# Key projections moved into the units of differential attention, and its values taken as 256 moving columns

## What is computed

```python
def diff_attention(q, k, v, cos, sin, lam_params, head_gain, lam_init):
    q = apply_rope(q, cos, sin)
    k = apply_rope(k, cos, sin)
    ...
        s = jnp.einsum('bqhcd,bkhcd->bhcqk', qb, k).astype(jnp.float32) * scale
        s = jnp.where(kpos[None, :] <= qpos[:, None], s, NEG_INF)
        p = jax.nn.softmax(s, axis=-1)
        a = p[:, :, 0] - lam * p[:, :, 1]
        return jnp.einsum('bhqk,bkhe->bqhe', a.astype(v.dtype), v)
    ...
    o = rmsnorm(o, head_gain) * (1.0 - lam_init)

def nsa(q, k_cmp, v_cmp, k_slc, v_slc, k_win, v_win, gate_logits, ...):
    kc = compress(k_cmp, cmp_pos[0], cmp_w1[0], cmp_w2[0])
    vc = compress(v_cmp, cmp_pos[1], cmp_w1[1], cmp_w2[1])
    ...
    ks = apply_rope(k_slc, cos, sin)
    kw = apply_rope(k_win, cos, sin)
```

## Time and profile before

| | |
|---|---|
| time, median of 3 runs | 2116.81 us (2115.66 to 2120.5) |
| the profiled execution: time | 2119.69 us |
| the profiled execution: span | 2117.9 us |
| mean granted TensorE clock over the span | 0.986 |
| TensorE busy | 2023.9 us (96%) |
| VectorE, ScalarE, GpSimd busy | 1041.1, 815.1, 275.3 us |

### The profile page before, as it was taken

How to read it: one execution, slowest core, us unless ns; L and a number is a source line. 1 busy time by engine, 2 the same in 40 slices (tenths; PEclk the granted TensorE clock), 3 DMA queues, 4 the chain that set the end, 5 groups by cost and what they waited for, 6 DMA issues and landing times.

```text
span 2117.9 us, 25446 instructions
## 1 busy us (share of the span) xinstructions
PE 2023.9 (96%) x10148; PEld 1697.5 (80%) x10148; DVE 1041.1 (49%) x1606; ACT 815.1 (38%) x1482; POOL 275.3 (13%) x272
## 2 busy tenths in 40 slices
PE   6999999999999999999998899989989999999998
PEld 6887888888878888888886788777777888888886
DVE  5665555555353222335545665856665543222333
ACT  5442443333243222324225643455554333222332
POOL 1001000000000000000013432266763000000000
PEclk9999999999999999999999899999999999999999
DMA  5232333333323332332541043311115423333332
GB/s 190 80 100 60 101 99 100 94 95 100 100 81 99 100 92 97 100 99 80 149 130 40 1 150 123 90 46 49 42 46 170 139 64 116 99 100 93 96 100 70
DMA packets 58982, 200.12 MB, mean 94 GB/s; under 512 B 8081, under 2 KB 8113, under 8 KB 58481
## 3 DMA queue, kind: packets, MB, share of 16 engines
q1 hardware_dynamic: 53936, 178.29, 27.3%
q0 software_dynamic: 4928, 20.21, 2.8%
HBM read 181.16 MB, written 8.39 MB: 90 GB/s over the span
## 4 chain that ended last, share of the span: by engine, by line
PE 75%; DVE 7%; ACT 5%; POOL 5%; issue 3%; DVEq 2%; DMA 1%; POOLq 1%; SPq 0%; ACTq 0%
PE ps L636 24%; PE ps L637 24%; PE ps L638 24%; POOL PU L592 5%; DMA raw<-in_w_all 1%; DVE Wl L1699 1%; DVE XN L1739 1%; DVE HTl L1748 1%; PE ps L1086 1%; ACT Pb L1367 1%; DVEq L2257 1%; POOLq L581 1%; PE ps L1002 1%; ACT XN L1240 1%; ACT Wh L1207 1%
## 5 line engine op out<-in xcount | busy, mean ns | idle before, releaser
L1699 DVE TENSOR_TENSOR Wl<-raw,Wh 128x1024 fp32r<-128x1024 f32 x307 | 377.4, 1232 | 766.3 <-ACT Wh L1207 764.9
L636 PE MATMUL ps<-HTh,Wh 128*128 128x512 f32 (+1 forms) x1696 | 642.8, 379 | 14.9 <-DVE HTl L1748 10.5
L637 PE MATMUL ps<-HTl,Wh 128*128 128x512 f32 (+1 forms) x1696 | 636.8, 375 | 0.0
L638 PE MATMUL ps<-HTh,Wl 128*128 128x512 f32 (+1 forms) x1696 | 636.7, 375 | 0.0
L1207 ACT CAST Wh<-raw 128x1024 fp32r<-128x1024 f32 x307 | 321.7, 1052 | 802.0 <-DMA raw<-in_w_all 802.0
L636 PEld LDWEIGHTS ps<-HTh,Wh 128*128 128x128 f32 x1696 | 321.7, 190 | 73.0 <-issue 13.6
L638 PEld LDWEIGHTS ps<-HTh,Wl 128*128 128x128 f32 x1696 | 321.1, 189 | 57.8
L637 PEld LDWEIGHTS ps<-HTl,Wh 128*128 128x128 f32 x1696 | 321.4, 190 | 55.1
L636 PE MATMUL ps<-Wh,Yh 128*128 128x512 f32 x528 | 206.1, 390 | 4.3 <-DVE Yl L1875 4.3
L638 PE MATMUL ps<-Wh,Yl 128*128 128x512 f32 x528 | 205.5, 389 | 0.0
L637 PE MATMUL ps<-Wl,Yh 128*128 128x512 f32 x528 | 205.4, 389 | 0.0
(11 more groups left out here) (281 smaller groups left out, 2382.2 us busy)
## 6 DMA issues: line engine op xcount, KB each, us to landing
raw<-in_w_all SPq DMA_DIRECT2D x307, 512.0 KB, 3.6
swp_d<-qkd SPq DMA_DIRECT2D x64, 64.0 KB, 2.9
g_dram<-gst SPq DMA_DIRECT2D x16, 256.0 KB, 4.0
ring<-g_dram POOLq DMA_DIRECT2D x16, 256.0 KB, 3.6
gpre<-in_g_pre POOLq DMA_DIRECT2D x5, 512.0 KB, 4.0
X<-in_x SPq DMA_DIRECT2D x4, 512.0 KB, 5.2
swp_r<-qkr SPq DMA_DIRECT2D x16, 128.0 KB, 2.3
cw1k<-in_cw POOLq DMA_DIRECT2D x1, 2048.0 KB, 8.1
```

The costliest lines, as they stand in the source:

```text
L636: tensor.matmul(dst, a_hi, b_hi, start=start, stop=False)
L637: tensor.matmul(dst, a_hi, b_lo, start=False, stop=False)
L638: return tensor.matmul(dst, a_lo, b_hi, start=False, stop=stop)
L1699: vector.tensor_tensor(Wl[:, s, :], raw[:, s, :], Wh[:, s, :], ALU.subtract).then_inc(w_lo, 1)
```

## The change

- `Vst` holds each block's high and low part side by side, and `values` takes a block as one matmul of 256 columns (high A x [high V, low V]) and one of 128 (low A x high V). The result of high x low lands in the second 128 columns of the bank, and VectorE adds it to YD (`add_low`), after ScalarE's `da_out`. All units use bank 6, which `add_low` frees.
- `da_out(t)` moves from ScalarE's iteration t + 3 to t + 2.
- The four nsf chunks are 32 steps of one `three` each in bank 7: six behind `scores(1)`, then one behind each of the units 0 to 25. Their results (`nsf_out`) and the splits that stood with them move into iterations 2, 10, 18 and 26.
- The first V, Q and K casts stand between the first exps instead of ahead of them, and TensorE's wait on all eight banks ahead of attention is gone.
- `kcv`, `kraw`, `swp_n`, `DSQ`, `hid4` and `CS0` get other places. So the key swaps are issued after the first nst chunk, the vhl casts wait for `ks_f`, the scaling of YD and its store come after the vhl parts, GpSimd builds both halves of cA ahead of the store, and ksh and ksl move from query chunks 0 and 1 to 4 and 5.

```diff
-    ("da", 0, [0] * 8, [16, 16, 16, 16, 16, 16, 16, 16]),
-    ("nsf", 4, [1, 1, 1, 1, 0, 0, 0, 0], [0] * 8),
+    ("nsf", 4, [0, 0, 0, 0, 0, 0, 0, 4], [0] * 8),
+    ("da", 0, [0] * 8, [16, 16, 16, 16, 16, 16, 32, 0]),
     ("nst", 3, [1, 1, 1, 1, 0, 0, 0, 0], [0] * 8),
...
-        Vst = at("Vst", -8, [P, 2, 2, SEQ], F32R)
+        Vst = at("Vst", -8, [P, 2, TT, 2, P], F32R)
...
-        DSQ = at("DSQ", 64, [P, TT, D])
+        DSQ = at("DSQ", 0, [P, TT, D])
...
-        kcv = at("kcv", 64, [P, 2, SEQ])
+        kcv = at("kcv", 88, [P, 2, SEQ])
...
-        hid4 = at("hid4", 68, [P, 2, 2, 4, 32])
-        kraw = at("kraw", 44, [P, 2, SEQ])
+        hid4 = at("hid4", 65, [P, 2, 2, 4, 32])
+        kraw = at("kraw", 92, [P, 2, SEQ])
...
-        swp_n = at("swp_n", 76, [P, 2, SEQ])
+        swp_n = at("swp_n", 80, [P, 2, SEQ])
...
-        CS = [at("CS0", 36, [P, 32, 32]), at("CS1", 52, [P, 32, 32])]
+        CS = [at("CS0", 67.75, [P, 32, 32]), at("CS1", 52, [P, 32, 32])]
...
+        FIRST_STEPS = 6
+
+        def nsf_ends(t):
+
+            done = FIRST_STEPS + t
+            return done // 8 - 1 if done % 8 == 0 and 8 <= done <= 32 else None
...
-                c = m - CHUNK0["nsf"]
-                if c in (2, 3) and on("nsf"):
-                    swap("nsf", c - 2, c, 0, kraw[:, c - 2, :], swp_n[:, c - 2, :])
+                if m == CHUNK0["nst"] and on("nsf"):
+                    for c in range(2):
+                        swap("nsf", c, 7, 2 + c, kraw[:, c, :], swp_n[:, c, :])
...
-                    by_tile = lambda a: a.rearrange("p (t n) -> p t n", t=TT)
-                    pool.tensor_tensor(by_tile(Vst[:, u, 1, :]), vd[:, :, span(it, 2 * P, head * P, P)],
-                                       by_tile(Vst[:, u, 0, :]), ALU.subtract).then_inc(st_lo, 1)
+                    pool.tensor_tensor(Vst[:, u, :, 1, :], vd[:, :, span(it, 2 * P, head * P, P)], Vst[:, u, :, 0, :],
+                                       ALU.subtract).then_inc(st_lo, 1)
...
-                for b in (6, 7):
-                    pl.wait_ge(full[b], FILLED["nsf"][b])
+                pl.wait_ge(full[6], FILLED["da"][6] + TOTAL)
...
-                pl.wait_ge(full[7], FILLED["nsf"][7])
...
-                for tt in range(TT):
-                    pl.wait_ge(da_fin, tt + 1)
-                    pl.dma_start(y_dram[tt], YD[:, tt, :]).then_inc(yd_out, 16)
                 def inputs(kv):
 
-                    pl.wait_ge(free[kv], FREED["nst"][kv])
+                    pl.wait_ge(free[7], FREED["nsf"][7] + kv + 1)
...
+                inputs(1)
+                pool.drain()
+                for tt in range(TT):
+                    pl.wait_ge(da_fin, tt + 1)
+                    pl.dma_start(y_dram[tt], YD[:, tt, :]).then_inc(yd_out, 16)
                 pl.wait_ge(yd_out, 16 * TT)
                 load(cw1v[:].rearrange("p j n -> p (j n)"), t["cw1"][1], in_cwv)
-                inputs(1)
-                pool.drain()
...
-                b = 6 + u
-                bank_free("da", b, t // 2)
+                b = 6
+                bank_free("da", b, t)
                 if t % 4 == 0:
                     pe.wait_ge(st_lo, 4 * (t // 4) + 4)
                 bank_free("da", 4 + u, t // 2 + 1)
                 for j in range(n):
                     a = slice(j * P, (j + 1) * P)
-                    last = three(ps[b][:, 0:P], ATdh[:, u, 0, a], ATdl[:, u, 0, a], Vst[:, t // 4 % 2, 0, a], Vst[:, t // 4 % 2, 1, a],
-                                 j == 0, j == n - 1)
+                    v = Vst[:, t // 4 % 2, j, :, :]
+                    tensor.matmul(ps[b][:, 0:2 * P], ATdh[:, u, 0, a], v.rearrange("p a n -> p (a n)"), start=j == 0, stop=False)
+                    last = tensor.matmul(ps[b][:, 0:P], ATdl[:, u, 0, a], v[:, 0, :], start=False, stop=j == n - 1)
                 last.then_inc(full[b], 1)
+
+            def nsf_steps(a, b):
+                for n in range(a, b):
+                    c, k = n // 8, n % 8
+                    w = weights(CHUNK0["nsf"] + c)
+                    if k == 0:
+                        bank_free("nsf", 7, c)
+                    q = slice(k * P, (k + 1) * P)
+                    last = three(ps[7][:], Wh[:, w, q], Wl[:, w, q], HTh[:, k, :], HTl[:, k, :], k == 0, k == KT - 1)
+                    if k == KT - 1:
+                        last.then_inc(w_used, 1)
 
             def attention():
                 scores(0)
                 scores(1)
+                nsf_steps(0, FIRST_STEPS)
                 for t in range(TOTAL):
                     if exists(t - 2):
                         values(t - 2)
                     if exists(t + 2):
                         scores(t + 2)
                     turn(t)
+                    if FIRST_STEPS + t < 32:
+                        nsf_steps(FIRST_STEPS + t, FIRST_STEPS + t + 1)
                 values(TOTAL - 2)
                 values(TOTAL - 1)
...
-                for b in range(8):
-                    pe.wait_ge(free[b], FREED["da"][b])
                 pe.wait_ge(st_zero, 1)
                 attention()
-            if on("nsf"):
-                for c in range(4):
-                    gemm_f("nsf", c, c)
...
+                pe.wait_ge(ks_lo, 1)
...
-                at_least(ac, full[6 + u], t // 2 + FILLED["da"][6 + u])
+                at_least(ac, full[6], FILLED["da"][6] + t - 1)
                 scalar.copy(ATdh[:, u, 0, 0:w], ps[4 + u][:, 0:w]).then_inc(at_hi, 1)
 
             def da_out(t):
-                u = t % 2
-
-                if t >= TOTAL - 2:
-                    filled("da", 6 + u, t // 2)
-                scalar.activation(YD[:, t % 4, span(0, 2 * P, t // 4 * P, P)], ps[6 + u][:, 0:P], ACT.Copy,
-                                  scale=rr[:, t % STEPS, 0:1]).then_inc(free[6 + u], 1)
+                filled("da", 6, t)
+                scalar.activation(YD[:, t % 4, span(0, 2 * P, t // 4 * P, P)], ps[6][:, 0:P], ACT.Copy,
+                                  scale=rr[:, t % STEPS, 0:1]).then_inc(y_part, 1)
+
+            def nsf_out(c):
+                chunk_done("nsf", c)
+                dst = kcv[:, c, :] if c < 2 else kraw[:, c - 2, :]
+                scalar.copy(dst, ps[7][:]).then_inc(free[7], 1)
+                split(CHUNK0["nsf"] + c + LEAD)
 
             def attention():
                 exps(0)
+                high_parts(0, 0, 1)
                 exps(1)
+                high_parts(0, 1, 0)
                 for t in range(TOTAL):
-                    if exists(t - 3):
-                        da_out(t - 3)
+                    if nsf_ends(t) is not None:
+                        nsf_out(nsf_ends(t))
+                    if exists(t - 2):
+                        da_out(t - 2)
                     high(t)
...
                         exps(t + 2)
-                for t in range(TOTAL - 3, TOTAL):
-                    da_out(t)
+                da_out(TOTAL - 2)
+                da_out(TOTAL - 1)
...
-                    scalar.copy(Vst[:, u, 0, :].rearrange("p (t n) -> p t n", t=TT), vd[:, :, span(it, 2 * P, head * P, P)]).then_inc(st_hi, 1)
+                    if head == 0:
+                        ac.wait_ge(free[6], FREED["da"][6])
+                    scalar.copy(Vst[:, u, :, 0, :], vd[:, :, span(it, 2 * P, head * P, P)]).then_inc(st_hi, 1)
 
 
...
             if on("da"):
-                ac.wait_ge(free[6], FREED["da"][6])
-                high_parts(0, 0, 1)
-                high_parts(0, 1, 0)
                 attention()
             if on("nsf"):
 
-                scalar.drain()
+                ac.wait_ge(free[6], FREED["da"][6] + TOTAL)
                 scalar.activation(DSQ[:], YD[:], ACT.Square).then_inc(da_sq, 1)
                 ac.wait_ge(da_ss, 1)
                 scalar.activation(hsd[:], hss[:], ACT.Sqrt, scale=1.0 / P, bias=eps[:]).then_inc(da_sd, 1)
-                for c in range(4):
-                    split(CHUNK0["nsf"] + c + LEAD)
-                    chunk_done("nsf", c)
-                    dst = kcv[:, c, :] if c < 2 else kraw[:, c - 2, :]
-                    scalar.copy(dst, ps[c][:]).then_inc(free[c], 1)
             if on("nst"):
                 for c in range(3):
                     split(CHUNK0["nst"] + c + LEAD)
...
+                ac.wait_ge(ks_f, 1)
...
                     query(c)
-                    if c == 0:
-                        ac.wait_ge(ks_f, 1)
+                    if c == 4:
...
+            def add_low(t):
+
+                ve.wait_ge(y_part, t + 1)
+                y = YD[:, t % 4, span(0, 2 * P, t // 4 * P, P)]
+                vector.scalar_tensor_tensor(out=y, in0=ps[6][:, P:2 * P], scalar=rr[:, t % STEPS, 0:1], in1=y,
+                                            op0=ALU.mult, op1=ALU.add).then_inc(free[6], 1)
+
             def attention():
...
+                    if exists(t - 2):
+                        add_low(t - 2)
                     if exists(t + 2):
                         maxima(t + 2)
+                    if nsf_ends(t) is not None:
```

(25 more changed lines are left out.)

1 line of the change is left out of this document (added).

## The result

The changed kernel takes 2122.67 us (median of 11 runs, 2119.71 to 2134.05). In the same comparison the kernel before takes 2117.02 us (11 runs, 2111.07 to 2121.14). The ratio is 1.0056, 95% interval 1.0039 to 1.0073. It is taken over the single runs and is not the ratio of the two medians, which is 1.0027. Forecast were 2104 us and a gain, so the sign was wrong, and the time is 8.7 us above the top of the range. The profiled execution has a span of 2120.5 us and a time of 2122.25 us. The changed kernel's runs fall in two groups: seven lie at 2119.7 to 2124.2 us and four at 2132.6 to 2134.1 us. The profile shown here is of the first; experiment 7 shows what parts them.

What follows compares the result with a forecast made beforehand. Attention was taken as bound by a loop through all three engines, not TensorE's work. Stretches go from 124 to 109 us, gain 15, less 2 for the wait and 0.1: 13 us, giving 2104 us, range 2091 to 2114.

Steps and rivals of the forecast that it cites:

- part 5: Behind attention: `cmp_hidden(0)` could start at 26.4 us, bank 0 comes free at 28.5, so TensorE waits 2 us.
- The second rival: Chain behind attention is later: kind 1 slowed, cw1v late, `cmp_hidden` waits 6 to 8 us; 2109 us, chance 0.18.
- Part 1: Value blocks on TensorE: each falls from 0.34 to 0.23 us, 8.6 us less work over 80 blocks.
- Parts 2 to 4: Attention with Key projection steps, `add_low` and single bank 6: 107 us instead of 100.
- my lap: One head's loop through VectorE, TensorE and ScalarE in attention: 12.1 to 12.2 us, 0.2 more than the 11.95 before.
- finished chunk: Bank 7 copy, cast and subtraction in four heads of attention: 2.4 us each, 9.7 us in all.
- Part 4: Attention's new lap: 8 laps of 97.6 us against 93.6 us of TensorE work, so the steps hide.
- the 1.5 us for stretches at the lower clock: Allowance added to attention's 107 us, less than the 4 us reckoned before because TensorE is busier.
- The loop closes up: Rival: in attention ScalarE's block and finished chunks fall into slack, VectorE alone bounds at 93 us; 2090 us, chance 0.15.
- The single bank decides: Rival: values wait for YD and `add_low` in every unit, 0.7 us 32 times, 22 us; 2124 us, chance 0.12.

Runs made afterwards that it cites:

- experiment 7: The changed kernel, unchanged, run again for a second profile; 2128.48 us, ratio 1.0056 to the kernel before.
- experiment 11: The changed kernel without the four GpSimd drains inside `inputs`; 2118.9 us, ratio 1.0031 to the kernel before.
- 10: The changed kernel with values as three 128-column matmuls, no `add_low`, tail reordered, nst in banks 2 to 5; 2103.73 us, ratio 0.9955 to before.
- Experiment 6: The changed kernel with nst in banks 2 to 5, YD scaling ahead of keys, YD stores and cw1v load ahead of cA's second half; 2107.5 us, ratio 0.9965.
- 2: The changed kernel with 34 unused 512-column matmuls filling the gap ahead of the first compression's wait for bank 0; 2122.8 us, ratio 1.0040.
- 12: 10 without the four GpSimd drains inside `inputs`; 2101.1 us, ratio 0.9954 to the kernel before.

## Why the prediction was wrong

**The step that failed is part 5, "TensorE waits 2 us".** The wait was 7.9 us, for three reasons.

- `cA` was placed at 5.5 to 22 us behind attention, beside kind 0 only. It ran from 12 to 29.5 us, beside both kinds. The reason could be read before: in the old trace, too, its sums came 7.21 and 8.46 us after GpSimd's last DMA issue. I had not asked why; experiment 11 shows that the drain holds them.
- The swaps landed 5.0 us after their issue, while cw1k and the weights were being loaded, and VectorE waited 3.4 us for them; I had them down as in time.
- Both kinds cost 4.5 us in their sums, and three of the four products ahead of the sums took 1.2 us instead of 0.7. ks_f came some 30 us behind attention instead of 25.

**What the working lacked altogether is the price of a wait in clock.** The matmuls behind it took 13.5 us instead of 7.0, and the next microseconds cost 1.6 us more. A wait of 7.9 us thus cost 16 us, and in the longer group of runs the second compression added 6.5 us. The second rival named this wait at "6 to 8 us in all" and still gave 2109 us, since it held no clock. The forecast span was 2105 us: 6 us more of wait, 6.5 and 1.6 of clock, and the untraced 1.3 make 2120.4, against 2120.5. That it closes so well is in part luck, since errors in attention cancel in it.

**Part 1, a value block at 0.23 us: right.** TensorE in time, changed kernel:

```profile
1190.72 0.34 PE L804 MATMUL ps<-Vst,ATdh 128*128 128x256 f32 x1
1190.89 0.22 PE L805 MATMUL ps<-Vst,ATdl 128*128 128x128 f32 x1
1190.95 0.34 PE L804 MATMUL ps<-Vst,ATdh 128*128 128x256 f32 x1
```

A block starts 0.23 us after the one before it, split 0.17 and 0.06. The work saved, though, was not what bound the loop: 10, without it, has the shorter heads.

**Parts 2 to 4, attention at 107 us: right in sum (108.3), wrong in its terms.** `add_low` was 0.345 us as bounded, but cost 1.3 us a lap (13.43 against 12.13) where my lap rose by 0.2 over before. A finished chunk cost 0.8 us (14.26 against 13.43), not 2.4. The errors, 8 x 1.2 = 10 us and 4 x 1.6 = 6 us, cancel in good part. The clock hid a third: with attention at full clock, before needs 92.3 us and not the 96 that I reckoned with. Part 4 also had the steps hide. They do not quite: with the old values (10) they and what came with them cost 6.3 us in six heads at full clock, although TensorE was busy for only 73.4 of 77.7 us. And the 1.5 us for stretches at the lower clock did not foresee the last 18 us at 0.81. That attention came out near 107 is luck as far as these terms go.

**The rivals.** "The loop closes up" didn't happen: VectorE waited 14.4 us for YD. "The single bank decides" was half right, in its place but not its size: 6.9 us of TensorE's waits, 12 of them, are for `add_low`, not 22 us. Neither decided the sign. Experiment 6 has the attention of the changed kernel and is faster than before (0.9965), so the sign lay behind attention; but its gain of 0.35% is smaller than the 0.6% forecast, and 10 shows that it would be a little larger without the new values (0.9955, with overlapping intervals). No single run separates the wait from the clock that follows it: the attempt (2) didn't keep the clock up. Nor do the runs part the order on VectorE from the order on GpSimd, or test the new places of `kcv`, `kraw` and `swp_n` by themselves.

## What to carry to other kernels

When a change pulls work forward out of a stretch, price the chain that this work used to cover, with each operation beside what now runs beside it, and ask of every idle time in the old trace what ends it, before it is on the path. A TensorE wait ahead of a run of narrow matmuls can cost twice its length, so put the wait elsewhere or shorten the chain before taking away its cover. And profile the baseline twice when its runs spread by 10 us: the one execution that the forecast stood on held nearly 8 us that were the clock's.

## What the runs showed of the hardware

- 64 matmuls of 62 columns, back to back, stayed at the lower clock level for 13.5 us (0.214 us apart) where they started there, and lost the upper one 1.7 us after their start in 2. In 12 it was lost in the 64-column matmuls just ahead of them, 3 us behind a wait of 0.7 us. In 512-column matmuls behind them the upper level was back after 3 us in the changed kernel (1294.3 to 1297.5) and after 5 us in 7. At the upper level starts were 0.11 us apart at 62 columns and at 128.
- A drain on GpSimd held its next operation until the DMAs that GpSimd had issued had landed: 8.0 to 13.8 us of idle time behind the last of a group of six, 0.2 to 0.4 us after its landing. Without the drain the operation started while the last load had 10 us to go (11), or 0.1 us behind the issue (12, second half of `cA`). What it waits for may be a 64 KB load that nobody needs yet.
- A 64 KB load behind a 2 MB one took 8.2 to 14.0 us to land, in the same place of the program in all fourteen traces.
- The two groups of run times of the changed kernel, 10 us apart, go with one stage, by one profile of each: whether the second compression gets the upper clock. The two profiles of the kernel before, 8 us apart, differ in the clock within attention. Of 12 only the longer group was profiled, with the second compression at the lower clock.
